# Attention heads 8 to 15 in another order on TensorE, ScalarE and VectorE

## The reference

```
qkv = (h @ w_qkv).reshape(Bsz, S, 3, N_HEADS, HEAD_DIM)      # S = 256, 16 heads of 64
q = rope(q, pos) * (HEAD_DIM ** -0.5)
k = rope(k, pos)
...
s_own = jnp.einsum('bhqd,bhjd->bhqj', qc, ko)
s_own = jnp.where(kpos <= qpos, s_own, NEG_INF)
p = jax.nn.softmax(...)
o = einsum(p, v)
return o @ w_o
...
x = x + moba_attention(h, moba_w_qkv[j], moba_w_o[j])
x = x + conv_ffn(rmsnorm(x, ffn_norm[i]), ffn_w_up[i], ffn_w_conv[i], ffn_w_down[i])
```

## Time and profile before

| | us |
|---|---|
| median of three runs | 1181.91 |
| lowest and highest of them | 1179.38, 1184.22 |
| the profiled execution, its device time | 1181.57 |
| its span in the trace | 1179.8 |

### The profile page before, as it was taken

How to read it: one execution, slowest core, us unless ns; L and a number is a source line. 1 busy time by engine, 2 the same in 40 slices (tenths; PEclk the granted TensorE clock), 3 DMA queues, 4 the chain that set the end, 5 groups by cost and what they waited for, 6 DMA issues and landing times.

```text
span 1179.8 us, 17165 instructions
## 1 busy us (share of the span) xinstructions
PE 1091.3 (93%) x6358; PEld 942.7 (80%) x6358; DVE 843.7 (72%) x1089; ACT 719.4 (61%) x954; POOL 74.6 (6%) x79
## 2 busy tenths in 40 slices
PE   7996696999999999898999999999999878999997
PEld 6884675787777877677987999998788668899996
DVE  5447577989999999867565666666767646767765
ACT  6468446888888888755434554455466655545553
POOL 1000200000000000011000110120000001111100
PEclk9997598999999999999999999999899989999999
DMA  9530153888888889743642545554433314555440
GB/s 372 195 125 1 38 202 126 314 327 329 325 343 324 340 327 351 296 149 137 211 170 100 212 167 212 180 192 162 144 141 107 107 36 161 214 197 194 163 157 36
DMA packets 33605, 232.64 MB, mean 197 GB/s; under 512 B 3856, under 2 KB 3984, under 8 KB 6032
## 3 DMA queue, kind: packets, MB, share of 16 engines
q1 hardware_dynamic: 32688, 229.98, 52.5%
q10 hardware_dynamic: 864, 1.93, 0.5%
HBM read 230.85 MB, written 1.05 MB: 197 GB/s over the span
## 4 chain that ended last, share of the span: by engine, by line
PE 74%; DVE 13%; ACT 8%; issue 3%; DMA 1%; POOL 1%; DVEq 0%; ACTq 0%; SPq 0%; POOLq 0%
PE bank L1783 11%; PE bank L1785 10%; PE bank L1784 10%; PE bank L2171 9%; PE bank L2173 9%; PE bank L2172 9%; DVE wlo L1069 5%; PE bank L2040 4%; PE bank L2041 4%; ACT whi L496 2%; PE bank L2024 2%; PE bank L2048 1%; DVE arena L1431 1%; PE bank L2089 1%; PE bank L2088 1%
## 5 line engine op out<-in xcount | busy, mean ns | idle before, releaser
L1069 DVE TENSOR_TENSOR wlo<-raw,whi 128x2048 fp32r<-128x2048 f32 x212 | 481.8, 2287 | 103.2 <-ACT whi L496 101.6
L496 ACT ACTIVATE whi<-raw 128x2048 fp32r<-128x2048 f32 x213 | 406.6, 1917 | 120.1 <-PE bank L2173 64.2
L2171 PE MATMUL bank<-xs,whi 128*128 128x256 f32 x896 | 250.8, 280 | 5.5 <-DVE wlo L1069 3.3
L2173 PE MATMUL bank<-xs,wlo 128*128 128x256 f32 x896 | 250.4, 280 | 0.0
L2172 PE MATMUL bank<-xs,whi 128*128 128x256 f32 x896 | 249.9, 279 | 0.0
L2171 PEld LDWEIGHTS bank<-xs,whi 128*128 128x128 f32 x896 | 168.4, 188 | 7.4 <-DVE wlo L1069 3.7
L2172 PEld LDWEIGHTS bank<-xs,whi 128*128 128x128 f32 x896 | 168.4, 188 | 0.8
L2173 PEld LDWEIGHTS bank<-xs,wlo 128*128 128x128 f32 x896 | 168.4, 188 | 0.0
L1783 PE MATMUL bank<-whi,rounded 128*128 128x512 f32 x344 | 140.8, 409 | 8.4 <-DVE rounded L1440 4.1
L1785 PE MATMUL bank<-whi,rounded 128*128 128x512 f32 x344 | 138.3, 402 | 0.0
L1784 PE MATMUL bank<-wlo,rounded 128*128 128x512 f32 x344 | 137.9, 401 | 0.0
(11 more groups left out here) (320 smaller groups left out, 1495.9 us busy)
## 6 DMA issues: line engine op xcount, KB each, us to landing
raw<-stream SPq DMA_DIRECT2D x215, 1024.0 KB, 4.8
arena<-finals ACTq DMA_DIRECT2D x3, 512.0 KB, 3.2
xres<-x_in SPq DMA_DIRECT2D x2, 512.0 KB, 4.3
raw<-stream SPq DMA_DIRECT2D x4, 256.0 KB, 6.2
out<-xn SPq DMA_DIRECT2D x4, 256.0 KB, 2.1
par<-params SPq DMA_DIRECT2D x1, 844.0 KB, 12.5
cst<-table SPq DMA_DIRECT2D x1, 502.0 KB, 9.0
arena<-p_in ACTq DMA_DIRECT2D x1, 256.0 KB, 3.8
```

Source lines behind the costliest of these rows:

```text
L496: act.activation(whi[:, s, :], raw[:, a, :], ACT.Copy).then_inc(S("high_done"), 1)
L1069: dve.tensor_tensor(wlo[:, s, :], raw[:, unit0 % RAW, :], whi[:, s, :].bitcast(F32), ALU.subtract)\
L2171: pe.matmul(o, whi[:, s, w], xhi[:, kk, :], start=first, stop=False, skip_group_check=True)
L2173: ins = pe.matmul(o, wlo[:, s, w], xhi[:, kk, :], start=False, stop=kk == 7, skip_group_check=True)
```

## The change

ACT's `weights` is cut in two, `exponentials` and `over_sum` (the division), and the loops over heads 8 to 15 are written in another order on three engines. PE makes the scores two heads ahead, starts each step with `turn_p(8 + i)`, and puts a W_O piece between it and `values(8 + i - 1)`; two W_O pieces now stand ahead of the first `turn_p`, and two pieces with u = 1 behind the loop move around. DVE makes the maxima one head ahead and V's low part (`v_low`) after them. The halves of W_O's units are split in other steps. Every instruction of before is still there once. The first loop (heads 0 to 7) and the other engines keep their order.

```diff
-            def weights(h):
+            def exponentials(h):
...
                 ins.then_inc(S("exp_done"), 1)
+
+            def over_sum(h):
+                b, rl = h % 3, V("rl")
                 act.wait_ge(S("rl_ready"), h + 1)
...
-            for i in range(10):
-                if i >= 2:
-                    pt_high(8 + i - 2)
+            for i in range(9):
                 if i < 8:
-                    weights(8 + i)
-                if i >= 3 and i % 2:
-                    o_high(4 + (i - 3) // 2)
-                if i in (1, 2, 5, 6):
-                    split_half(U_WO + 2 + i // 4, (i - 1) % 4)
+                    exponentials(8 + i)
+                if i >= 1:
+                    pt_high(8 + i - 1)
+                if i in (4, 6, 8):
+                    o_high(4 + (i - 4) // 2)
+                if i < 8:
+                    over_sum(8 + i)
+                if i in (0, 1, 5, 6):
+                    split_half(U_WO + 2 + i // 5, i % 5)
+            o_high(7)
             split_to(U_WO + 4)
...
-            v_low(1)
-            HALVES = {1: (U_WO + 1, 0), 2: (U_WO + 1, 1), 4: (U_WO + 2, 0), 6: (U_WO + 2, 1), 8: (U_WO + 3, 0)}
-            for i in range(10):
-                if i >= 2:
-                    pt_low(8 + i - 2)
+            maxima(8)
+            HALVES = {1: (U_WO + 1, 0), 2: (U_WO + 1, 1), 3: (U_WO + 2, 0), 5: (U_WO + 2, 1), 6: (U_WO + 3, 0),
+                      7: (U_WO + 3, 1)}
+            for i in range(9):
                 if i < 8:
-                    maxima(8 + i)
                     over_sums(8 + i)
-                if i >= 3 and i % 2:
-                    o_low(4 + (i - 3) // 2)
+                if i < 7:
+                    maxima(8 + i + 1)
+                if i == 0:
+                    v_low(1)
+                if i in (4, 6, 8):
+                    o_low(4 + (i - 4) // 2)
+                if i >= 1:
+                    pt_low(8 + i - 1)
                 if i in HALVES:
                     split_half(*HALVES[i])
-            split_half(U_WO + 3, 1)
+            o_low(7)
             split_to(U_WO + 4)
...
-            for i in range(10):
-                if i < 8:
-                    scores(8 + i)
-                if i >= 2:
-                    values(8 + i - 2)
-                if i == 4:
+            scores(8)
+            scores(9)
+            o_part(0, 0, (0, 1))
+            pieces = [(0, 0, 2), (0, 0, 3), (1, 0, 0), (1, 0, 1), (1, 0, 2), (1, 0, 3), (0, 1, 0), (0, 1, 1)]
+            for i, (c, u, k) in enumerate(pieces):
+                turn_p(8 + i)
+                if i < 6:
+                    scores(8 + i + 2)
+                if i == 2:
                     pe.wait_ge(S("v_ready"), 2)
-                if i < 8:
-                    o_part(i // 4, 0, (i % 4,))
-                else:
-                    o_part(0, 1, (i - 8,))
-                if 1 <= i < 9:
-                    turn_p(8 + i - 1)
+                o_part(c, u, (k,))
+                if i >= 1:
+                    values(8 + i - 1)
+            o_part(1, 1, (0,))
+            values(15)
+            o_part(1, 1, (1,))
             o_part(0, 1, (2, 3))
-            o_part(1, 1, all4, (0,))
-            o_part(1, 1, all4, (1,))
+            o_part(1, 1, (2, 3), (0,))
+            o_part(1, 1, (2, 3), (1,))
```

More of the change, by code:

```diff
@@ L902, in weights @@
                 b, sc = h % 3, bank[4 + h % 2]
-                nm, l, rl = V("nm"), V("l"), V("rl")
+                nm, l = V("nm"), V("l")
                 for t, w in ((1, slice(0, 256)), (0, slice(256, 384))):
@@ L935, in _ @@
                 if i < 8:
-                    weights(i)
+                    exponentials(i)
+                    over_sum(i)
                 if i % 2:
```

## The result

| | us |
|---|---|
| before, median of 4 runs beside it | 1182.45 (1179.38 to 1184.22) |
| after, median of 4 runs | 1167.87 (1164.91 to 1171.19) |
| ratio | 0.9885, 95% interval 0.9866 to 0.9904 |
| the profiled execution after: device time, span | 1166.92, 1165.1 |

The account below looks back on a forecast made before the run. The stage was held by engines waiting for each other, PE for DVE's `pt_low`. Stage 37.6 + 1.7 + 0.4 = 39.7 us, gain 16.4; less 2.2 (norm) and 1.2 (clock), 13.0 us: median 1168.9 us, range 1164.5 to 1175.5.

Parts of the forecast that it names:

- The bound: Heads 8 to 15: no engine short of capacity; PE waits 10.1 us before `values` for DVE's `pt_low`, plus low clock.
- PE's own work: Stage of heads 8 to 15: eight heads 13.9 us plus W_O's 16 pieces 23.7 us, 37.6 us at full clock.
- the 2.1 I took: PE's remaining stage waits: 1.7 us before `values` of heads 10, 12 and 14, 0.4 us before `scores(9)`.
- The clock in the stage: No wait above 1.1 us in the stage, so low clock put at nothing, from an earlier 17 us stretch at 1.00.
- Rival (b): Stage: clock keeps falling though waits are short, 7.6 us of low clock stay, 1176.5 us; chance 6%.
- The tail: Behind W_O's last piece: the norm comes later, losing 2.2 us, and a low clock after it costs 1.2 us.
- The two terms: Norm's transposes at E + 5.3 against 3.1, loss 2.2 us; low clock after PE's 4.2 us standstill, 1.2 us.
- FFN1: After the norm: same PE work, order and weight stream, so expected to move as a whole, keeping its 195 us.
- rival (d): FFN1 begins 13 us earlier and waits for weights from HBM, losing at most the whole gain, 1181.9 us; chance 2%.
- Rival (a): Stage: uneven steps, four costing 1 us more each, one wait lowering the clock (2.5 us), 1175.4 us; chance 15%.
- Rival (c): Stage: engines walk in series, 7.1 us a step, stage 70.6 us, time about 1200 us; chance 2%.
- The time: Whole kernel: 13.0 us gained, profiled execution 1168.6 us, median 1168.9 us; forecast's chance 75%.

Follow-up runs that it names:

- Squares: The changed kernel, with the high part of FFN1's second weight unit on ScalarE moved behind all four squares of the norm; 1167.69 us.
- units first: The changed kernel, with FFN1's first weight unit split ahead of the last bank 7 (ScalarE, VectorE) and its second unit's high part behind all four squares; 1165.38 us.

## Why the prediction was right, step by step

**The bound.** "The stage is held by who waits for whom" stands: with the same instructions it went from 56.1 to 39.9 us (39.7 predicted), and every change to the new order within the stage moved it. ScalarE's share alone, put into the old order, did not (56.1 us).

**PE's own work** was put at 37.6 us and is 39.9 - 1.7 = 38.2. The 0.6 too few were offset, by luck, by waits that were smaller than the 2.1 I took: 0.24 before `scores(9)` (0.4 predicted), 0.32, 0.32 and 0.78 before `values` of heads 10, 12 and 14 (0.3, 0.3, 1.1). The last is the longest, as said.

**The clock in the stage** stayed at 1.00, as taken from the earlier trace rows. But those rows were thin ground for it: the stretch at 1.00 ends at 953.9, 1.1 us after the wait of 2.07 us, and this is the next row of the same view:

```profile
953.90:957.40 3.50, 3.50 (x14) 2.93 (x13) 1.48 (x3) 2.77 (x8) 0.00 (x0) 0.52 0.17 26
```

So rows 3 don't show that a wait of 2.07 us leaves the clock up; what bears the term out are the runs. Rival (b) is out for this order: in no trace of a kernel with the new order, nine of them, was it lower in the stage. The experiment of the scores one head ahead is the hardest case: ten waits of 0.57 to 1.47 us, 11.7 of 50.9 us, at 1.00. By what the Trainium skill says of another kernel, which the prediction weighed as a rule (TensorE: Matmul & The Clock Gate, section A second HAM failure mode: psum-queue depth-cycling), short idle gaps between groups of matmuls that go round the banks can make the clock swing; these two traces don't show it.

The gain of 16.2 us in the stage is thus 9.3 us of waits (10.94 - 1.66) and, as the rest, 6.9 of clock, which agrees with the 13.6 us at half the clock that the stage held before (6.8 us, if PE was busy in all of it). The experiments show that it is no sum of separate edits: ScalarE's share alone gives nothing, and taking the second head of lead away costs 11.1 of the 16.2 us, with the rest in place but for DVE's bank 7 part. The division's place is worth 1.9, the two pieces ahead 2.4 (1.0 of it given back behind the stage), V's low part 0.9. PE's order alone and VectorE's alone were not run.

**The tail** was put at 2.2 + 1.2 = 3.4 us and cost 3.1. Its mechanism is confirmed row by row: the low part of the unit ends at 960.33, E - 1.98 (predicted E - 1.95), ACT's second unit runs from E to E + 1.9, the squares of half 1 begin at 964.13 and 964.75, E + 1.8 and E + 2.4. Squares and units first take 1.9 and 2.8 us of it away. The two terms were mis-sized in opposite directions. DVE scales the second tile from 967.60, so its transposes come at 968.1 at the earliest, E + 5.8 where I had 5.3: 2.7 us. The low clock lay from 966.4, just ahead of the transposes, to 969.8, still within them, so it cost 0.4 us and not 1.2 (from the first transposes to FFN1 970.47 - 966.53 = 3.94 us, and 968.80 - 965.21 = 3.59 in units first, at 1.00). This is its row in the windows view:

```profile
966.40:969.80 3.40, 3.27 (x16) 3.22 (x16) 1.38 (x4) 0.83 (x3) 1.61 (x4) 0.50 0.00 0
```

That it ended so early was luck, since in four other traces of the new order, with the same 4.2 us of wait, it lasted 6.8 us and reached into FFN1, which took 195.5 to 195.6 us there: the term was then 1.3 us. The tail's 3.1 us, near the 3.4 predicted, is thus also a sum of two errors.

**FFN1** moved as a whole (194.6 us, 194.7 before), so rival (d) is out. Rival (a) asked for 1 us more in each of four steps; none had it. Rival (c), the walk in series at 7.1 us a step, is out: from one head's transposes to the next's PE took 2.4 to 3.8 us. It was approached only where I took the lead of the scores away, at 4.2 to 5.9.

**The time.** The stage's 16.2 less the tail's 3.1 are 13.1 us, against 13.0 predicted: that is what the mechanism gives. The 14.6 us between the medians hold 1.5 more, and the 10.0 of the later session 3 less; the traces show nothing of the change in either: between the first two profiled executions 1.5 us lie ahead of the stage, and in the later session the stage and the tail of after are the same as in the first. That the median came out within 1.0 us of the forecast is therefore partly luck.

## What to carry to other kernels

Where a dependent chain goes round several engines, compare the work of the bounding engine in one step with the chain's latency between two of its own instructions, and put each instruction of a slower walker directly behind the event that releases it, on every engine that the chain passes: ScalarE's reorder alone gave nothing here, and a lead of one head too few, with VectorE's low part behind the maxima of the next head, took the gain back. Then follow the saved time to the next serial place: weight units that had been hidden by the stage's length stood in front of the norm, and moving one of them into idle time of the same engines, and the high part of another behind the squares, gave another 3 us.

## What the runs showed of the hardware

- Two traces of one kernel were 10.3 us apart, and the difference lay ahead of the stage, whose start wandered from 917.1 to 928.8 us over the traces; the stage itself agreed to 0.5 us. Parts of a kernel are compared from their own start. In these two traces (scores one head ahead) PE is busy for 852.3 and 861.5 us up to the stage, with the same 4798 records, and DVE and ACT are busy alike to 0.5 us, so it is the matmuls that ran longer. The mean clocks of the two spans, 0.968 and 0.964, stand for 37.5 and 42.6 us, half of the difference at most; what makes the rest stays open.
- All stages whose longest wait was at most 1.8 us ran at 1.00, whatever the sum of their waits (up to 11.7 us); all four traces with waits of 2.1 us or more in the stage had 10.2 to 13.6 us of low clock in it. But it is no rule for a single wait: in the first trace of ScalarE's order alone the clock stayed at 1.00 after waits of 2.60 and 2.59 us and fell in one of 3.40 (from 962.4 on), in its second trace it fell already in one of 2.59 (from 951.5 on), and in the second trace of before a low stretch of 3.4 us began at 949.2, 1.2 us behind a wait of 1.46.
- In and just behind the stage the low clock lasted 3.4, 6.8 or 10.2 us at a time, and what it cost hung on where it fell: 0.4 us under the transposes behind a wait of 4.2 us, and 0.9 to 1.0 us more where it reached into FFN1 (195.5 to 195.6 instead of 194.6 us, in four traces).
